# Summing squares over partitions with GpSimd instead of TensorE for the former tile's output and heads 0 and 1, in a fused HGRN2 and pooling step

## What is computed

```
h = rmsnorm(x, norm_g)
z = h @ w_in                       # split into q, f, i, g_a, u, g_b, m_a, m_b
o, s_new = hgrn2_chunked(q, 1 - f, i, log f, s0)    # 4 heads of 128 x 128 state, s0 = 0 for the prompt
o = rmsnorm(o, hgrn_norm_g) * silu(g_a)             # over the 128 channels of a head
pooled = multiscale_pool(u)        # windows 2, 4, 8, 16
y_a = o @ w_proj_a;  y_b = (pooled @ w_pool * pool_scale * silu(g_b)) @ w_proj_b
out = x + (sigmoid(m_a) * y_a + sigmoid(m_b) * y_b) @ w_out
y = rmsnorm(out, final_norm_g)     # over the 1024 channels
```

## Time and profile before

| what | value |
|---|---|
| median of 3 runs | 1374.38 us (1374.23 to 1375.24) |
| profiled execution, span from its first to its last instruction | 1372.1 us |
| median of the runs less that span | 2.3 us |
| TensorE busy | 1359.5 us, 99% |
| VectorE busy | 932.0 us, 68% |
| ScalarE busy | 685.6 us, 50% |
| GpSimd busy | 198.4 us, 14% |
| granted TensorE clock, mean | 0.998 of full speed |

### The profile page before, as it was taken

The page is one execution under the profiler, slowest core; times in us unless marked ns, Lnnn a source line. Parts: engine busy times, 40 slices in busy tenths (PEclk is TensorE's granted clock), DMA queues, the critical chain, the costliest instruction groups (busy, mean ns, idle before and its releaser), DMA issues.

```text
span 1372.1 us, 21266 instructions
## 1 busy us (share of the span) xinstructions
PE 1359.5 (99%) x8272; PEld 1345.2 (98%) x8272; DVE 932.0 (68%) x1642; ACT 685.6 (50%) x992; POOL 198.4 (14%) x200
## 2 busy tenths in 40 slices
PE   9999999999999999999999999999999999999997
PEld 7999999999999999999999999999999999999997
DVE  7899655668975456788844567987445689964443
ACT  6565444355664344556643445665433556653332
POOL 2003021110031211001212110012220200130001
PEclk9999999999999999999999999999999999999999
DMA  6544533246535333465363335653532476534338
GB/s 207 140 131 127 208 122 122 94 130 200 143 108 212 118 123 107 129 193 147 98 222 110 121 110 144 171 156 126 189 122 96 136 170 205 178 108 173 118 100 94
DMA packets 140259, 195.91 MB, mean 143 GB/s; under 512 B 83712, under 2 KB 100480, under 8 KB 138496
## 3 DMA queue, kind: packets, MB, share of 16 engines
q1 hardware_dynamic: 140160, 194.56, 47.1%
HBM read 174.91 MB, written 19.61 MB: 142 GB/s over the span
## 4 chain that ended last, share of the span: by engine, by line
PE 92%; DVE 5%; DMA 1%; issue 1%; ACT 1%; SPq 0%; DVEq 0%; ACTq 0%
PE Z L519 29%; PE Z L521 28%; PE Z L520 28%; DVE wlo L1038 1%; DMA wraw<-w_all 1%; PE B L575 1%; PE B L668 1%; PE B L658 1%; PE B L552 0%; DVE xres L1441 0%; DVE snew L1198 0%; DVE h_b L1078 0%; PE B L519 0%; PE B L521 0%; PE B L520 0%
## 5 line engine op out<-in xcount | busy, mean ns | idle before, releaser
L1038 DVE TENSOR_TENSOR wlo<-wraw,whi 128x1024 fp32r<-128x1024 f32 x280 | 367.0, 1311 | 299.7 <-ACT whi L796 299.5
L519 PE MATMUL Z<-hhi,whi 128*128 128x416 f32 x1576 | 552.7, 351 | 0.0
L520 PE MATMUL Z<-hlo,whi 128*128 128x416 f32 x1576 | 549.4, 349 | 0.0
L521 PE MATMUL Z<-hhi,wlo 128*128 128x416 f32 x1576 | 549.4, 349 | 0.0
L796 ACT ACTIVATE whi<-wraw 128x1024 fp32r<-128x1024 f32 x280 | 295.9, 1057 | 425.2 <-PE Z L521 353.0
L519 PEld LDWEIGHTS Z<-hhi,whi 128*128 128x128 f32 x1576 | 296.0, 188 | 0.9 <-issue 0.6
L520 PEld LDWEIGHTS Z<-hlo,whi 128*128 128x128 f32 x1576 | 296.0, 188 | 0.5
L521 PEld LDWEIGHTS Z<-hhi,wlo 128*128 128x128 f32 x1576 | 295.9, 188 | 0.3
L521 PE MATMUL Z<-mhi,wlo 128*128 128x416 f32 x320 | 112.3, 351 | 0.0
L520 PE MATMUL Z<-mlo,whi 128*128 128x416 f32 x320 | 111.9, 350 | 0.0
L519 PE MATMUL Z<-mhi,whi 128*128 128x416 f32 x320 | 111.5, 348 | 0.0
(11 more groups left out here) (252 smaller groups left out, 1555.2 us busy)
## 6 DMA issues: line engine op xcount, KB each, us to landing
wraw<-w_all SPq DMA_DIRECT2D x280, 512.0 KB, 3.5
xres<-xT SPq DMA_DIRECT2D x5, 1664.0 KB, 7.5
xin<-xT SPq DMA_DIRECT2D x4, 1664.0 KB, 7.8
yT<-xres SPq DMA_DIRECT2D x4, 1664.0 KB, 8.9
v_blocks<-h_vt SPq DMA_DIRECT2D x80, 52.0 KB, 3.1
vtm<-v_blocks SPq DMA_DIRECT2D x20, 192.0 KB, 3.9
ktm<-k_blocks SPq DMA_DIRECT2D x20, 192.0 KB, 3.6
k_blocks<-kt SPq DMA_DIRECT2D x64, 52.0 KB, 1.9
```

The source lines that it names most:

```text
L519: pe.matmul(out, wh, xh, start=first, stop=False)
L520: pe.matmul(out, wh, xl, start=False, stop=False)
L521: return pe.matmul(out, wl, xh, start=False, stop=final)
L1038: dve.tensor_tensor(wlo[n % RING][:], raw(t, n)[:], whi[n % RING][:].bitcast(F32), ALU.subtract).then_inc(wlo_made, 1)
```

## The change

Three edits. The sums of squares over partitions of the former tile's output, and of heads 0 and 1 in every tile, are made by one GpSimd instruction each (`partition_all_reduce`, which gives the sum over partitions to every partition), in place of the split by DVE and the matmul by PE. The products of the zero state with the queries of group 0 are left out in the first tile. Semaphores follow. Heads 2 and 3, the squares of x, and the output of the last tile stay as they were. Cut to its core:

```diff
+POOLED = 2
+SUMMED = 4 - POOLED
...
-        if _s == 4 * _h + 12:
+        if _s == 4 * _h + 12 and _h >= POOLED:
             B5_USES.append(("ssq", _h))
...
-B5_USES.append(("yssq", 0))
...
                     if s == 6 and last:
-                        sp.wait_ge(ysplit, t)
+                        sp.wait_ge(yall_made, t)
                         sp.dma_start(s0[0][:], s_in[0]).then_inc(s0_landed[0], 16)
...
-                    if s == base + 12:
-                        pe.wait_ge(ssplit, nth(t, H, h))
+                    if s == base + 12 and h >= POOLED:
+                        pe.wait_ge(ssplit, nth(t, SUMMED, h - POOLED))
...
-                if s == YNORM and not first(t):
-                    y_squares(t - 1, False)
...
-                for g in range(NG):
+                for g in range(1 if first(t) else 0, NG):
                     pe.matmul(B5[:, g * P:(g + 1) * P], s_all[:, g, :],
...
             def head_sum(t, h):
-                act.wait_ge(ssq_done, nth(t, H, h))
-                act.activation(rst[:], B5[:, 0:T], ACT.Ln, bias=eps_t[:], scale=1.0 / P).then_inc(b5_read, 1)
+                if h < POOLED:
+                    act.wait_ge(sall_made, nth(t, POOLED, h))
+                    act.activation(rst[:], rst[:], ACT.Ln, bias=eps_t[:], scale=1.0 / P).then_inc(sln_made, 1)
+                else:
+                    act.wait_ge(ssq_done, nth(t, SUMMED, h - POOLED))
+                    act.activation(rst[:], B5[:, 0:T], ACT.Ln, bias=eps_t[:], scale=1.0 / P).then_inc(b5_read, 1)
...
                         if s == 4 * h + 9:
                             act.wait_ge(o_done, nth(t, H, h))
-                            act.wait_ge(ssplit, t * H + h)
-                            if first(t) or last:
+                            if 0 < h <= POOLED:
+                                act.wait_ge(sall_made, t * POOLED + h)
+                            else:
+                                act.wait_ge(ssplit, t * SUMMED + max(h - POOLED, 0))
+                            if first(t) or last or h < POOLED:
                                 act.activation(osq[:], B5[:, 0:T], ACT.Square).then_inc(osq_made, 1)
...
             def y_norm(t):
-                act.wait_ge(yssq_done, t + 1)
-                act.activation(yrs[:], B5[:, 0:T], ACT.Ln, bias=eps_t[:], scale=1.0 / D).then_inc(b5_read, 1)
+                act.wait_ge(yall_made, t + 1)
+                act.activation(yrs[:], yrs[:], ACT.Ln, bias=eps_t[:], scale=1.0 / D).then_inc(yln_made, 1)
...
-                    if s == YNORM - 2 and not first(t):
-                        y_split(t - 1, False)
...
-                    if s % 4 == 2 and 10 <= s <= 22:
+                    if s % 4 == 2 and 10 + 4 * POOLED <= s <= 22:
...
                     if s == 0 and not first(t):
                         y_sum(t - 1, KD - 1)
+                        pool.wait_ge(yacc_made, t * (KD - 1))
+                        pool.partition_all_reduce(yrs[:], yacc[:], P, bass.bass_isa.ReduceOp.add).then_inc(yall_made, 1)
+                    for h in range(POOLED):
+                        if s == 4 * h + 10:
+                            pool.wait_ge(osq_made, nth(t, H, h))
+                            pool.wait_ge(t1_made, t * H + h)
+                            pool.partition_all_reduce(rst[:], osq[:], P, bass.bass_isa.ReduceOp.add).then_inc(sall_made, 1)
```

More of the change, by code:

```diff
@@ L112 @@
 RC_FIRST = G + 1
-YNORM = 4
 SPLIT_SOONER = [4 * _h + 5 for _h in range(H)]
@@ L287, in step_kernel @@
         p_done, o_done, ssq_done, mix_done = sem("p_done"), sem("o_done"), sem("ssq_done"), sem("mix_done")
-        xssq_done, yssq_done = sem("xssq_done"), sem("yssq_done")
+        xssq_done = sem("xssq_done")
         whi_made, sq_made, sg_made, sb_made = sem("whi_made"), sem("sq_made"), sem("sg_made"), sem("sb_made")
@@ L307, in step_kernel @@
         ssplit, xsplit, ysplit = sem("ssplit"), sem("xsplit"), sem("ysplit")
-        halves_added, xfolded, yfolded = sem("halves_added"), sem("xfolded"), sem("yfolded")
+        halves_added, xfolded = sem("halves_added"), sem("xfolded")
         ssplit_hi, xsplit_hi, ysplit_hi = sem("ssplit_hi"), sem("xsplit_hi"), sem("ysplit_hi")
@@ L312, in step_kernel @@
         xacc_made, yacc_made, masks = sem("xacc_made"), sem("yacc_made"), sem("masks")
+        yall_made, yln_made, sall_made, sln_made = sem("yall_made"), sem("yln_made"), sem("sall_made"), sem("sln_made")
         smasks, so_done, so_made, kh_made, split_k, split_v = (sem("smasks"), sem("so_done"), sem("so_made"), sem("kh_made"),
@@ L628, in sample_states, with y_squares @@
                 mm.then_inc(so_done, 1)
[L630 to L644, removed]
+            def y_squares(t):
+                pe.wait_ge(ysplit, 1)
+                pe.wait_ge(b5_read, b5_done(t, "ssq", H - 1))
+                pe.wait_ge(ybm_made, nth(t, G, G - 1))
+                for bank, c in zip((B5, B6), TAIL):
+                    pe.matmul(bank[:, c], ones_r[:], sqh[:, c], start=True, stop=False)
+                    pe.matmul(bank[:, c], ones_r[:], sql["y"][:, c], start=False, stop=False)
+                for i, (bank, c) in enumerate(zip((B5, B6), TAIL)):
+                    pe.wait_ge(tail_squared, i + 1)
+                    pe.matmul(bank[:, c], ones_r[:].bitcast(F32), ysq[(KD - 1) % 2][:, c], start=False,
+                              stop=True).then_inc(tail_summed, 1)
             def sum_squares(bank, what, final=True):
@@ L738, in tile @@
                 if last:
-                    y_squares(t, True)
+                    y_squares(t)
             def first_unit():
@@ L848, in head_sum @@
             def head_sum(t, h):
-                act.wait_ge(ssq_done, nth(t, H, h))
-                act.activation(rst[:], B5[:, 0:T], ACT.Ln, bias=eps_t[:], scale=1.0 / P).then_inc(b5_read, 1)
+                if h < POOLED:
[4 more added lines that the diff above has]
+                    act.activation(rst[:], B5[:, 0:T], ACT.Ln, bias=eps_t[:], scale=1.0 / P).then_inc(b5_read, 1)
             def head_norm(t, h):
-                act.wait_ge(b5_read, b5_done(t, "ssq", h))
+                if h < POOLED:
+                    act.wait_ge(sln_made, nth(t, POOLED, h))
+                else:
+                    act.wait_ge(b5_read, b5_done(t, "ssq", h))
                 act.activation(rst[:], rst[:], ACT.Exp, scale=-0.5).then_inc(rst_made, 1)
@@ L902, in tile @@
                             act.wait_ge(t1_made, t * H + h)
-                            if not (first(t) or last):
+                            if not (first(t) or last or h < POOLED):
                                 act.activation(rst[LOWER], B5[UPPER, 0:T], ACT.Square).then_inc(osq_made, 1)
@@ L1286, in tile @@
                                           ALU.subtract).then_inc(pml_made, 1)
-                    if s % 4 == 2 and 10 <= s <= 22:
+                    if s % 4 == 2 and 10 + 4 * POOLED <= s <= 22:
                         h = (s - 10) // 4
+                        n = nth(t, SUMMED, h - POOLED)
                         dve.wait_ge(osq_made, nth(t, H, h))
-                        if h:
-                            dve.wait_ge(ssq_done, nth(t, H, h - 1))
+                        if h > POOLED:
+                            dve.wait_ge(ssq_done, n - 1)
                         elif not first(t):
-                            dve.wait_ge(yssq_done, t)
+                            dve.wait_ge(xssq_done, t + 1)
                         if first(t) or last:
-                            split_squares(osq, "head", (ssplit_hi, ssplit), nth(t, H, h))
+                            split_squares(osq, "head", (ssplit_hi, ssplit), n)
                         else:
                             dve.tensor_tensor(osq[LOWER], osq[LOWER], rst[LOWER], ALU.add).then_inc(halves_added, 1)
-                            dve.wait_ge(halves_added, (t - 1) * H + h + 1)
-                            stack_squares(osq, (ssplit_hi, ssplit), nth(t, H, h))
+                            dve.wait_ge(halves_added, n - SUMMED)
+                            stack_squares(osq, (ssplit_hi, ssplit), n)
                     if s == XNORM - 2 and not last:
                         dve.wait_ge(xacc_made, nth(t, KD - 1, KD - 2))
-                        dve.wait_ge(ssq_done, nth(t, H, H - 1))
+                        dve.wait_ge(ssq_done, nth(t, SUMMED, SUMMED - 1))
                         fold_squares(xacc, xsq[0], (xsplit_hi, xsplit), t + 1, xfolded)
@@ L1397, in tile @@
                 if last:
-                    y_split(t, True)
+                    y_split(t)
                     dve.wait_ge(acc_done, acc_ready(t, "out", KD - 1))
@@ L1403, in tile, with y_split @@
                     output(t, range(KD))
[L1405 to L1415, removed]
+            def y_split(t):
+                dve.wait_ge(yacc_made, nth(t, KD - 1, KD - 3))
+                dve.wait_ge(ssq_done, nth(t, SUMMED, SUMMED - 1))
+                split_squares(yacc, "y", (ysplit_hi, ysplit), 1)
```

2 lines of the change are left out of this document (1 added, 1 removed).

## The result

The kernel after takes 1378.16 us (median of 6 runs, 1376.66 to 1379.91); before, in the same comparison, 1374.25 us (1373.25 to 1375.24). The ratio is 1.0028, with a 95% interval from 1.0018 to 1.0037: slower by 3.9 us, where I had forecast 4.4 us less. Its profiled execution took 1377.11 us, with a span of 1375.4. Of all the experiments' runs a single one is far off and left out of its ratio: 2754.97 us, one of the 11 of the kernel with the zero-state edit alone.

A forecast was written before the change was run, and what follows sets the result against it. PE's stream of matmuls was taken to bound every tile; removed sums and zero-state products gave 4.4 us, so span 1372.1 - 4.4 = 1367.7, plus 2.3 for the median: 1370.0 us. Range 1368.4 to 1374.5, rival 1 left out.

The forecast's parts named there:

- What leaves PE: PE's matmul stream: sums for the output and heads 0 and 1, plus zero-state products, leave it, saving 4.4 us.
- POOL in time: POOL's 14 reductions, taken as 7.6 us each, finish before ACT, SP or PE waits; windows 9.9 to 17.2 us.
- Rival 1: POOL's reductions take 27.4 us each and come late for ACT and PE: slower, 1455 us; chance 0.15.
- I cost this at nothing: both engines run beside PE: DVE loses splits and the output's fold, ACT squares heads 0 and 1 in one instruction: relief counted as nothing.
- so they delay nothing of its own: POOL does nothing between 287.6 and 373.3 us in tile 1, so the reductions delay none of POOL's own work.
- rival 2: Last tile: POOL and DVE slow each other or SP is late, PE waits 2 to 3 us: 1372.5 us; chance 0.08.
- The waits named as signs: ACT waiting on POOL, with PE waits on `ktm` or `wlo`: rival 1; PE wait only past 1110 us: rival 2.

## Why the prediction was wrong

- **What leaves PE: right in four tiles of five.** 4.4 us by the sum, 4.0 without the reductions. L532's successor has 6 records, L648's and L649's 4, the zero state's 112. The start-to-start distance of 0.19 us was the price, not the length of 0.35. In the last tile 0.8 us is given back to waits for DVE even without a reduction; the sum had no such term.
- **POOL in time: right, the duration not.** I took 7.6 us, measured 2.7 to 3.0. They began at 295.6, 328.5 and 354.3 us in tile 1; I had said 288, 327 and 351, without the pause of 5.9 us. Rival 1, with 1455 us, had nothing for it.
- **The failed step: "I cost this at nothing: both engines run beside PE", with "so they delay nothing of its own".** I followed every wait that the change adds, but none of its instructions' effect on an engine that doesn't wait for it. The term missing in the sum is nine holds of DVE of 1.6 us and one of 0.9, worth 8.0 us at PE with what follows them. The earlier trace rows held the warning, an add at 0.95 us and one at 1.96. I used them as bounds for POOL's duration, and for rival 2, and never as a price on DVE. And I misread the 0.95 us as "alone": DVE runs beside that add of 373.29 too, and this time DVE pays. In the kernel before:

```profile
373.39 1.26 DVE L1139 TENSOR_TENSOR q<-h_q,dec 128x384 f32<-128x384 f32 x1
```

The same product takes 0.55 us at 330.57, where POOL stands still. So the trace of before already priced a hold, at 0.7 us for an add of one microsecond, and a reduction of unknown length should have been given one too.
- **Rival 2 had the mechanism, not the place nor the size.** "POOL and DVE slow each other" is what happened, but I expected it in the last tile only, and no worse than the gain. The last tile did lose 2.9 us, near its 2 to 3, with 0.8 of it not from the reductions; the first lost 3.9, which no case had. I had looked for DVE's density only where PE already waited; before, DVE was busy in tile 0 for 4.67 of the 5 us from 90 to 95.
- **The waits named as signs.** "A PE wait that appears only past 1110 us would mean rival 2": it appeared at 97 us as well. The range, 1368.4 to 1374.5, had its upper end at an even result, because no case let the reductions cost more than they save except by being late.

## What to carry to other kernels

In these runs work moved to GpSimd was charged to VectorE too, a head's reduction in the kernel after with 0.9 to 1.6 us. So besides its deadline, write down which VectorE instruction runs beside it, whether that reads SBUF, and how much idle time VectorE has before the next engine misses it. If a reduction must run, start it where VectorE works on PSUM or waits, even if that is later; here 3 to 10 us of delay in an unhurried sum were worth some 7 us of kernel. A trial with the same GpSimd instruction on data that nobody needs, beside the untouched kernel, shows that there is a cost, if not its full size (4.6 us here, against 8.0).

## What the runs showed of the hardware

- A reduction over 128 partitions of 416 columns took 2.7 us on POOL (up to 3.0 where an instruction of DVE still ran as it began), and held DVE for the first 1.7 us of it, by the ten `wlo` of the kernel with the later start.
- DVE's running instruction kept its 0.59 us, while the reduction that began beside it was longer by 0.3: 3.0 us.
- Held were instructions of DVE with one SBUF input too: TENSOR_SCALAR from 0.49 to 2.07 us, COPY from 0.21 to 1.86. Those with an input from PSUM kept their 0.59 and 0.28 us.
- An addition on POOL beside DVE cost DVE 0.53 us on average, a reduction in a row of twelve 1.4 us.
- Each reduction for the output, which follows an addition, was preceded, in each run that has it, by 5.6 to 6.4 us in which POOL waited for nothing that the profile shows.
- A wait of 2.3 us at PE was followed by a granted clock of 0.83 in the windows from 95 to 105 us, and one of 1.9 us, with heads 0 and 1 alone on POOL, by 0.82 and 0.84. One of 1.6 us, beside the reductions that nobody waits for, left it at 1.00. Two waits close together, of 0.9 and 1.0 us, were followed by 0.68 in one kernel, and two of 0.8 and 1.0 us left 1.00 in another.
